# Other distances between the slots of the two weight rings in SBUF

## The reference, cut to what matters

```python
# two layers: modulation, input projection, attentions, output projection
shift, scale, gate = jnp.split(silu(c) @ w_ada[l] + b_ada[l], 3, axis=-1)
h = rms(x, norm_w[l]) * (1.0 + scale[:, None]) + shift[:, None]
u = h @ w_in[l]                      # (256 or 512 rows) x 2048 x 6208
...                                  # three kinds of attention on parts of u
x = x + gate[:, None] * ((y * silu(z)) @ w_out[l])
# then one mixer layer
z = h @ w_in_2                       # 256 x 2048 x 12304
merged = sigmoid(m_a) * (y_a @ w_proj_a) + sigmoid(m_b) * (y_b @ w_proj_b)
x = x + rmsnorm(merged @ w_out)
# cross attention with a memory of 256 rows, then
hid = conv(h @ ffn_w_up)             # 256 x 2048 x 11264
x = x + rmsnorm((gelu_gate(hid)) @ ffn_w_down)
```

## Time and profile before

| | |
|---|---|
| median of three runs | 3809.06 us |
| lowest, highest | 3808.15, 3813.33 us |
| profiled execution, its own time | 3810.96 us |
| its span, first to last instruction | 3809.2 us |
| TensorE matmuls busy | 3581.1 us, 94% |
| VectorE busy | 2015.6 us, 53% |
| ScalarE busy | 1674.3 us, 44% |
| casts (827) and subtractions (827) | 863.9 us and 1010.4 us |
| moved by DMA | 577.49 MB, a mean of 152 GB/s |
| mean granted TensorE clock | 0.973 |

### The profile page before, as it was taken

How to read it: one execution, slowest core, us unless ns; L and a number is a source line. 1 busy time by engine, 2 the same in 40 slices (tenths; PEclk the granted TensorE clock), 3 DMA queues, 4 the chain that set the end, 5 groups by cost and what they waited for, 6 DMA issues and landing times.

```text
span 3809.2 us, 46319 instructions
## 1 busy us (share of the span) xinstructions
PE 3581.1 (94%) x18672; PEld 2952.3 (78%) x18672; DVE 2015.6 (53%) x3121; ACT 1674.3 (44%) x2723; POOL 68.0 (2%) x118
## 2 busy tenths in 40 slices
PE   7899999999998898999899999999999799999998
PEld 1677778887776777778777787866778599999887
DVE  1666654344466845643355544445455566666544
ACT  2323344444422423445545444444545655544443
POOL 1200000000020000000000000000000000000000
PEclk8999999999999999999999999999999899999999
DMA  9653321233365455323355565644556355566565
GB/s 358 198 155 111 105 58 54 57 107 103 104 174 174 149 177 177 90 66 103 95 173 161 165 185 174 193 116 153 186 177 197 101 170 184 184 183 183 189 204 171
DMA packets 351045, 577.49 MB, mean 152 GB/s; under 512 B 25316, under 2 KB 131060, under 8 KB 348912
## 3 DMA queue, kind: packets, MB, share of 16 engines
q1 hardware_dynamic: 344512, 549.47, 46.7%
q0 software_dynamic: 6320, 25.06, 2.3%
HBM read 570.26 MB, written 4.19 MB: 151 GB/s over the span
## 4 chain that ended last, share of the span: by engine, by line
PE 56%; DVE 4%; ACT 3%; DMA 2%; issue 1%; DVEq 0%; SPq 0%; ACTq 0%
PE ps L709 35%; PE ps L1604 13%; PE ps L1286 1%; DMA raw_ring<-in_w_in_dram 1%; ACT w_hi L672 1%; DVE w_lo L678 1%; PE ps L1198 1%; PE ps L1084 1%; PE ps L1171 1%; PE ps L1180 0%; PE ps L746 0%; PE ps L1477 0%; PE ps L1482 0%; DMA raw_ring<-in_w_proj_b_dram 0%; PE ps L1194 0%
## 5 line engine op out<-in xcount | busy, mean ns | idle before, releaser
L678 DVE TENSOR_TENSOR w_lo<-raw_ring,w_hi 128x1024 fp32r<-128x1024 f32 (+1 forms) x827 | 1010.4, 1224 | 1143.5 <-ACT w_hi L672 1142.4
L672 ACT CAST w_hi<-raw_ring 128x1024 fp32r<-128x1024 f32 (+1 forms) x827 | 863.9, 1047 | 1259.3 <-PE ps L709 531.6
L709 PE MATMUL ps<-w_hi,r_a 128*128 128x512 f32 x3552 | 1295.1, 404 | 60.8 <-DVE f_arena L2823 20.1
L709 PE MATMUL ps<-w_lo,r_a 128*128 128x512 f32 (+1 forms) x2624 | 1031.7, 393 | 0.0
L709 PE MATMUL ps<-w_hi,r_b 128*128 128x512 f32 (+1 forms) x2272 | 853.0, 395 | 9.0 <-issue 4.4
L709 PEld LDWEIGHTS ps<-w_hi,r_a 128*128 128x128 f32 x3552 | 678.7, 191 | 228.2 <-issue 61.4
L709 PEld LDWEIGHTS ps<-w_lo,r_a 128*128 128x128 f32 x2624 | 503.7, 192 | 103.5 <-issue 7.9
L709 PEld LDWEIGHTS ps<-w_hi,r_b 128*128 128x128 f32 x2272 | 436.3, 192 | 104.1 <-issue 4.6
L1604 PE MATMUL ps<-r_a,w_hi 128*128 128x256 f32 x2816 | 509.0, 284 | 0.0
L1604 PEld LDWEIGHTS ps<-r_a,w_hi 128*128 128x128 f32 x2816 | 440.8, 193 | 0.0
L1604 PE MATMUL ps<-r_a,w_lo 128*128 128x256 f32 x1408 | 399.2, 284 | 0.0
(11 more groups left out here) (338 smaller groups left out, 2949.5 us busy)
## 6 DMA issues: line engine op xcount, KB each, us to landing
raw_ring<-in_w_in_dram SPq DMA_DIRECT2D x386, 512.0 KB, 3.7
raw_ring<-in_ffn_w_up_dram SPq DMA_DIRECT2D x176, 512.0 KB, 3.7
raw_ring<-in_w_ada_dram SPq DMA_DIRECT2D x128, 512.0 KB, 3.9
raw_ring<-in_w_out_dram SPq DMA_DIRECT2D x96, 512.0 KB, 3.7
raw_ring<-in_ffn_w_down_dram SPq DMA_DIRECT2D x88, 512.0 KB, 4.4
gla_arena<-in_w_ada_dram SPq DMA_DIRECT2D x64, 512.0 KB, 8.4
raw_ring<-in_w_proj_b_dram SPq DMA_DIRECT2D x32, 512.0 KB, 3.6
raw_ring<-in_w_proj_a_dram SPq DMA_DIRECT2D x16, 512.0 KB, 3.6
```

The lines of the kernel that those rows point to most:

```text
L672: nc.scalar.copy(WH[:, ph.s_slot(i, j), 0:n], RAW[:, ph.raw_slot(i, j), 0:n]).then_inc(hi_ready, 1)
L678: nc.vector.tensor_tensor(WL[:, ph.raw_slot(i, j), 0:n], RAW[:, ph.raw_slot(i, j), 0:n], WH[:, ph.s_slot(i, j), 0:n].bitcast(F32), ALU.sub ...
L709: mm = nc.tensor.matmul(PS[:, t, a:z], X(x, k, t), W[w][:, kk * cols + a:kk * cols + z], start=(k == 0 and q == 0), stop=(c == len(js) - 1 ...
```

## The change

The slots of the ring of high parts lie 1,024 + 32 floats apart, 4,224 bytes; those of the raw ring 1,024 + 16, 4,160 bytes. What a slot holds, and the numbers of slots, stay. The ring of high parts begins where it did; the raw ring begins 384 bytes later and ends 704 bytes behind big_end. vec_t and ada_t follow there, 704 and 320 bytes later than before; b_ada_t moves in among the small tensors ahead of the arenas, and those allotted after it move by 384 bytes. f_arena, r_a and r_b keep their addresses.

```diff
 SLOT = 1024
+HI_PITCH, RAW_PITCH = SLOT + 32, SLOT + 16
...
         big_end = (base + 53200 * 4) // 2048 * 2048
-        raw_off = big_end - 4 * RAW_SLOTS * SLOT
-        hi_off = raw_off - 4 * SPLIT_SLOTS * SLOT
+        hi_off = big_end - 4 * (RAW_SLOTS + SPLIT_SLOTS) * SLOT
+        raw_off = hi_off + 4 * SPLIT_SLOTS * HI_PITCH
+        raw_end = raw_off + 4 * RAW_SLOTS * RAW_PITCH
...
-        RAW = place("raw_ring", RAW_SLOTS * SLOT, F32, offset=raw_off).rearrange("p (s n) -> p s n", s=RAW_SLOTS)
-        WL = place("w_lo", RAW_SLOTS * SLOT, F32R, offset=raw_off).rearrange("p (s n) -> p s n", s=RAW_SLOTS)
-        WH = place("w_hi", SPLIT_SLOTS * SLOT, F32R, offset=hi_off).rearrange("p (s n) -> p s n", s=SPLIT_SLOTS)
+        RAW = place("raw_ring", RAW_SLOTS * RAW_PITCH, F32, offset=raw_off).rearrange("p (s n) -> p s n", s=RAW_SLOTS)
+        WL = place("w_lo", RAW_SLOTS * RAW_PITCH, F32R, offset=raw_off).rearrange("p (s n) -> p s n", s=RAW_SLOTS)
+        WH = place("w_hi", SPLIT_SLOTS * HI_PITCH, F32R, offset=hi_off).rearrange("p (s n) -> p s n", s=SPLIT_SLOTS)
         CN = place("consts", C_N)
-        VT = place("vec_t", 116, F32, offset=big_end)
-        BAT = place("b_ada_t", 96, F32, offset=big_end + 480)
+        VT = place("vec_t", 116, F32, offset=raw_end)
+        BAT = place("b_ada_t", 96)
...
-        ADA = place("ada_t", LAYERS * 96, F32, offset=big_end + 864).rearrange("p (l f s) -> p l f s", l=LAYERS, s=2)
+        ADA = place("ada_t", LAYERS * 96, F32, offset=raw_end + 480).rearrange("p (l f s) -> p l f s", l=LAYERS, s=2)
```

More of the change, by code:

```diff
@@ L150, in build @@
         RIO = place("gla_rinv", 8).rearrange("p (t h) -> p t h", t=2)
-        assert at[0] <= f_off and big_end + 864 + 4 * LAYERS * 96 <= base + 53200 * 4, at[0]
+        assert at[0] <= f_off and raw_end + 480 + 4 * LAYERS * 96 <= base + 53200 * 4, at[0]
         RA = place("r_a", 8192, F32R, offset=ra_off)
```

## The result

The changed kernel takes 3825.05 us, median of five runs (3818.05 to 3833.26), beside 3808.15 us (3804.29 to 3813.33) for the kernel before: a ratio of 1.0048, 95% interval 1.0035 to 1.006, about 17 us slower. The forecast was 3809.5 us and a range up to 3818.

A forecast was written before the change was run, and what follows sets the result against it. TensorE's matmuls, busy 94% of the span, were taken as the bound. The profiled 3810.96 us plus 0 to 1, with the timed median 1.9 us below the profile, gave 3809.5 us, range 3802 to 3818.

The forecast's parts named there:

- the multiply-adds: VectorE's multiply-adds over a raw slot, 740 to 755 ns in all 420 executions; the change was taken to cost zero.
- the landings: Arrival of loads in raw slots, 3.7 us; a longer landing was bounded at 0.19 us per load, taken as zero to 1 us in all.
- The slower-loads rival: Loads into raw slots off 256-byte boundaries pay one more piece per packet, 0.19 us per load waited for: 3820 us, chance 0.06.
- The small tensors: b_ada_t, vec_t, ada_t and those moved with them, read in a few short operations of mostly fixed duration: zero effect.
- part (1): High slots 4,224 bytes apart: zero for casts, subtractions and all matmuls; up to 12 us gain and 4 us loss allowed.
- part (2): Raw slots 4,160 bytes apart, starting 12,672 bytes above the high ring: the same zero for the engines.
- the last 740 us: Last stages, with up: five slots hide a load's landing and longer transfers fit, so their time was to stay unchanged.
- The rival on the clock: Clock falls come at other moments: 3 to 6 us either way, 3804 or 3814; counted within no effect, chance 0.88.
- the flat 389 ns: Last-stage matmuls had 389 ns as smallest, median and largest duration, read as no cost from meetings in SBUF.
- the 13.3 ns above one column a cycle: Remainder of 120.0 ns for 256 columns after 0.417 ns a column, taken as fixed in two stages using the rings differently.
- The closing sentence of the prediction: It would be wrong if alignment to 4,096 or 256 bytes gives what was taken for normal speed; no size given.
- The aliasing rival: Slots at one place modulo 4,096 collide in attention stages and new pitches undo it: up to 12 us gain, 3798 us, chance 0.06.

The follow-up runs named there:

- 112 bytes: Up product's activations moved 112 bytes further in r_a, rings moved 256 bytes as a whole, against the kernel before: 3779.77 us, ratio 0.9926.
- 192 bytes: TensorE alone, 256 columns, moving operand at 192 bytes, stationary at 0: 113.3 or 117.8 ns. In the kernel, up activations 192 bytes further: 3780.19 us, ratio 0.9935.
- the kernel with 64 bytes: Up product's activations moved 64 bytes further in r_a, rings moved 256 bytes as a whole, against the kernel before: 3794.72 us, ratio 0.9964.

## Why the prediction was wrong

*What held.* VectorE's and ScalarE's operations, the multiply-adds and the landings were costed at zero, and they are unchanged. The slower-loads rival falls: landings stay at 3.7 us, the DMA share at the same rate stays 0.60 in up, and the packets of the three long stretches differ by 1.6 ns at most. By the rule on unaligned descriptors in the Trainium skill, "DMA: Bandwidth & Descriptors", section "How a descriptor splits into AXI transactions", the loads would have cost an estimated 5% more if it held for writes into SBUF, which the page doesn't say; with four slots in five off a 256-byte boundary no such thing is seen. The small tensors cost nothing.

*The step that failed* is part (1), with part (2) as far as TensorE reads the raw ring: "Effect taken: zero ... for all matmuls", with a loss allowed of 4 us. Measured is +4.4 ns for each of the 512-column ring matmuls of the two long stretches and -1.6 ns for those of up. There are 9,600 of the first by the groups of before (those of the earlier trace rows and the smaller ones). Over all stages their mean went from 227.8 to 231.1 ns only, because in the attention stages they had 228 to 229 before, so the paces are worth an estimated 9,600 x 3.3 = 32 us less 4,176 x 1.6 = 7, 25 us. The medians grew by 17, and the span by 11 beside a clock that gave back up to 11. That the rest was hidden in stages where TensorE isn't what is waited for is likely and not shown. The sentence that the last 740 us stand still in every case fell with this step: up gained 6.7 us and the last stage lost 4.7. The rival on the clock was at work too, in the direction that hid part of the loss.

*How the reading misled.* I took the flat 389 ns as proof that places don't matter. But in that layout every ring slot and every stationary operand stood at the same place modulo 256 bytes. A quantity that never varies can't show its price. The rows said only that this one placement has one pace, while casts and loads come and go beside it, which does exclude the other engines (theory B) and nothing more. I also read the 13.3 ns above one column a cycle as fixed, because two stages shared it. Both shared the placement too; in the fastest state of 256 columns it is 6.7 ns, and in the slow ones of 512 columns 20. The closing sentence of the prediction named this hole, an alignment that gives what I take for normal speed, but no chance and no price went with it. A rival with 6.7 ns more on 9,600 matmuls, 64 us as an upper bound, would have had a place in the range.

*The aliasing rival* had the sign of the effect turned round. Equal places modulo 4,096 were not a collision to be undone but, for 512 columns, the best placement that was measured. For 256 columns it was right in a way that I hadn't priced: up was held at 120.0 ns by it, and with the differences that the rings came to it was 118.4 in the mean.

*The page on ports.* The Trainium skill, "SBUF — State Buffer", section "Who interferes with whom", gives TensorE two read ports, one for the moving operand and one for weight loads, and calls them independent. That the other engines don't disturb TensorE agrees with the runs here, which have the paces of TensorE alone to 0.1 ns in the last stage. That the two reads of TensorE are independent doesn't agree: with nothing else at work the pace goes from 226.7 to 234.4 ns with the difference of their places. The measurement decides; whether it is the ports that meet, or something behind them, no run tells.

*What stays open.* Which part of the hardware makes the two reads depend on each other isn't shown, nor why 256 columns have several states. The paces lie 6.67 ns apart (226.7 and 233.3; 113.3 and 120.0), 16 columns at 2.4 GHz, with others between. The 3 ns in the mean that ring matmuls have above 226.7 near other products were not explained by the identity's place. And the single-state behaviour of 112 bytes rests on four starts and six executions.

## What to carry to other kernels

Where TensorE sets the pace with one weight load for each matmul, the offset of the moving operand less that of the stationary one, modulo 256 bytes, with both at multiples of 32 bytes, is a parameter worth 3% of a 512-column matmul and 6% of a 256-column one. Keep it at zero for 512 columns of this kind, and measure it for others with a kernel that holds nothing but matmuls. A layout in which everything is equally placed gives a flat row that proves nothing about placement: before costing a move of addresses at zero, look for rows in which the address differs.

## What the hardware showed that was not expected

With TensorE alone, float32 operands in one-pass form and 2.4 GHz granted: with both places at multiples of 32 bytes, 226.7 ns for 512 columns at equal places and 228.8 to 234.4 at others, 120.0 ns for 256 columns at equal places and 113.3 to 120.0 at others. At finer places the paces go up to 237.7 ns for 512 columns, with both operands at 4 bytes, and up to 129.7 in one case of 256. At one and the same placement, 192 bytes, 113.3 or 117.8 ns by what ran before, each keeping on over the 40 matmuls of a case; in the kernel with 64 bytes 117.8 ns holds through all 4,176 matmuls, 491.84 us. The places of 4,352 bytes and 4,096 bytes of pitch give the same stage times to 0.01 us.
